# Last tile of a decoder layer: uneven gate columns, and a last norm shared by two engines and stored from two queues

## The reference, cut to what matters

```python
ffn = peer(x, ...)                                   # rows gathered from a table of 16384 experts
x = layer_norm(DEEPNORM_ALPHA * x + ffn, ln2_g, ln2_b)
gate = sigmoid(x @ ple_wgate + ple_bgate)            # 1024 x 1024
ple = gate * (p @ ple_wproj)                         # 256 x 1024
x = layer_norm(DEEPNORM_ALPHA * x + ple, ln3_g, ln3_b)
```

## Time and profile before

| what | us |
|---|---|
| time, median of 3 runs | 1459.02 (1455.46 to 1459.13) |
| the profiled execution, its time | 1458.8 |
| its span, first to last instruction | 1456.8 |
| mean granted TensorE clock | 0.886 |
| busy: PE / DVE / ACT / POOL | 1133.8 / 1084.4 / 934.7 / 602.7 |

### The profile page before, as it was taken

How to read it: one execution, slowest core, us unless ns; L and a number is a source line. 1 busy time by engine, 2 the same in 40 slices (tenths; PEclk the granted TensorE clock), 3 DMA queues, 4 the chain that set the end, 5 groups by cost and what they waited for, 6 DMA issues and landing times.

```text
span 1456.8 us, 18836 instructions
## 1 busy us (share of the span) xinstructions
PE 1133.8 (78%) x6787; PEld 889.4 (61%) x6787; DVE 1084.4 (74%) x2601; ACT 934.7 (64%) x1605; POOL 602.7 (41%) x533
## 2 busy tenths in 40 slices
PE   8999999988779877786666986777567775687666
PEld 3557777666667767665545565565555565566554
DVE  1388777769778886778747778877877787687867
ACT  2245678679878877766646666667655765666652
POOL 1034444334443434434424444554344444444551
PEclk9999999999889988898857988998879987778888
DMA  9589999999999999999999999999999999999991
GB/s 365 234 348 426 426 426 425 428 426 426 426 426 409 426 425 416 426 427 426 428 426 427 417 423 425 417 419 426 427 425 424 405 427 425 426 419 403 426 425 74
DMA packets 88359, 591.88 MB, mean 406 GB/s; under 512 B 9566, under 2 KB 14342, under 8 KB 19659
## 3 DMA queue, kind: packets, MB, share of 16 engines
q0 software_dynamic: 74128, 536.90, 88.0%
q1 hardware_dynamic: 14138, 53.79, 9.1%
HBM read 588.56 MB, written 2.10 MB: 405 GB/s over the span
## 4 chain that ended last, share of the span: by engine, by line
DMA 43%; PE 31%; ACT 10%; DVE 9%; POOL 3%; issue 3%; SPq 0%; POOLq 0%; DVEq 0%
DMA arena<-in_uv,ids 42%; PE ps L1051 12%; DVE arena L1609 6%; ACT arena L1256 5%; PE ps L763 4%; POOL arena L561 3%; PE ps L582 3%; PE ps L949 3%; PE ps L876 2%; ACT actv L1251 2%; PE ps L593 2%; ACT gel L1248 1%; ACT L1310 1%; ACT L1302 1%; PE ps L657 1%
## 5 line engine op out<-in xcount | busy, mean ns | idle before, releaser
L561 POOL DMA_INDIRECT arena<-in_uv,ids x512 | 589.8, 1152 | 787.3 <-PE ps L1051 664.4
L1051 PE MATMUL ps<-ident,arena 128*128 128x128 f32 x4076 | 618.9, 311 | 296.9 <-ACT arena L1256 296.0
L1051 PEld LDWEIGHTS ps<-ident,arena 128*128 128x128 f32 x4076 | 539.8, 161 | 395.3 <-ACT arena L1256 335.1
L1609 DVE CUSTOM_DVE_ANT_1 arena<-arena 128x1024 f32<-128x1024 f32 x384 | 468.5, 1225 | 207.5 <-DMA arena<-in_uv,ids 204.3
L1256 ACT ACTIVATE arena<-arena,actv 128x1024 f32<-128x1024 f32 x511 | 554.1, 1131 | 0.0
L1248 ACT ACTIVATE gel<-hid 128x2 f32<-128x2 f32 (+1 forms) x256 | 51.9, 203 | 406.7 <-DVE hid L1609 404.5
L1609 DVE CUSTOM_DVE_ANT_0 arena<-arena 128x1024 f32<-128x1024 f32 x128 | 155.4, 1224 | 63.3 <-DMA arena<-in_uv,ids 62.2
L1251 ACT ACTIVATE actv<-gel,gates 128x1 f32<-128x1 f32 x511 | 122.8, 287 | 8.4
L763 PE MATMUL ps<-arena 128*128 128x128 f32 x992 | 122.4, 285 | 0.0
L763 PEld LDWEIGHTS ps<-arena 128*128 128x128 f32 x992 | 120.5, 202 | 0.0
L876 PE MATMUL ps<-arena 128*128 128x384 f32 x192 | 65.9, 486 | 0.0
(11 more groups left out here) (226 smaller groups left out, 972.2 us busy)
## 6 DMA issues: line engine op xcount, KB each, us to landing
arena<-in_wq SPq DMA_DIRECT2D x20, 1024.0 KB, 9.0
arena<-in_uv,ids POOLq DMA_INDIRECT x517, 12.3
arena<-in_w_out SPq DMA_DIRECT2D x2, 2048.0 KB, 12.0
arena<-in_w_gate SPq DMA_DIRECT2D x1, 4096.0 KB, 17.9
arena<-in_w_out SPq DMA_DIRECT2D x3, 1024.0 KB, 13.5
arena<-in_w_k SPq DMA_DIRECT2D x4, 512.0 KB, 7.0
arena<-in_w_q SPq DMA_DIRECT2D x2, 1024.0 KB, 10.4
arena<-in_w_gv SPq DMA_DIRECT2D x1, 2048.0 KB, 12.0
```

The lines of the kernel that those rows point to most:

```text
L561: nc.gpsimd.indirect_dma_start(out=rows[:, c % RING, 0:n], out_offset=None, in_=a["uv"][:, :], in_offset=bass.IndirectOffsetOnAxis(ap=ids[ ...
L1051: i = mm(ps[:, run_bank(r) + k // 4, (k % 4) * P:(k % 4 + 1) * P], rows[:, c % RING, D + k * P:D + (k + 1) * P], ident[:, :], is_transpose ...
L1609: v.tensor_tensor_reduce(out=r, in0=r, in1=x1[t], scale=1.0, scalar=0.0, op0=ALU.mult, op1=ALU.add, accum_out=hid[:, i, c:c + 1]).then_inc ...
```

## The change: what it does

Three things, all in the tail of the last tile.

First, the four column groups of the gate, of 256 columns each, become groups of 320, 320, 256 and 128 columns (`LAST_COLS`), for the gate product, `gate_args`, the sigmoid and `add_embedding`. The instructions keep their number and order. The embedding is read through a view over two neighbouring banks, since columns 320 to 640 cross a bank's border.

Second, the last norm is cut at column 768 (`SPLIT`). VectorE centres columns 0 to 767 in one operation before it waits for the root, and rescales them in one operation after. GpSimd does columns 768 to 1023 in four operations, each waiting for the one before: subtract the mean and times g before the factor is known, times the factor and plus b after.

Third, the store: SyncE stores columns 0 to 767 in one transfer (384 KB), ScalarE's queue stores columns 768 to 1023 (128 KB), in place of SyncE's two of 512 columns (256 KB each).

```diff
--- before.py
+++ after.py
@@ -33,6 +33,8 @@
 
 RING = 8
 GRP = 2
+LAST_COLS = (0, 320, 640, 896, D)
+SPLIT = 768
 NG = TOPK // GRP
 HALF = D // 2
 REST = S - P
@@ -424,6 +426,12 @@
         ple_used = sem("ple_used")
         last_var = sem("last_var")
         last_root = sem("last_root")
+        last_mean_ready = sem("last_mean_ready")
+        last_rstd_ready = sem("last_rstd_ready")
+        last_centred = sem("last_centred")
+        last_kept = sem("last_kept")
+        last_a_ready = sem("last_a_ready")
+        last_b_ready = sem("last_b_ready")
         out_ready = sem("out_ready")
         out_done = sem("out_done")
 
@@ -512,8 +520,9 @@
             store(TAILS[1], 1)
             for u in range(28, NU):
                 load_wq(u)
-            for i in range(2, NT):
-                store(TAILS[i], i)
+            store(TAILS[2], 2)
+            sp.wait_ge(last_a_ready, 1)
+            sp.dma_start(out[0, TAILS[-1] * P:(TAILS[-1] + 1) * P, 0:SPLIT], x2[TAILS[-1]][:, 0:SPLIT]).then_inc(out_done, 16)
             sp.wait_ge(out_done, 2 * 16 * NT)
 
         @block.gpsimd
@@ -571,6 +580,17 @@
                     in_offset=bass.IndirectOffsetOnAxis(ap=ids[:, (NU - 1) % 4, c:c + 1], axis=0),
                     element_offset=PART,
                 ).then_inc(late_in[c - LATE], 16)
+
+            part = x2[TAILS[-1]][:, SPLIT:D]
+            pool.wait_ge(last_mean_ready, 1)
+            nc.gpsimd.tensor_scalar(part, part, aggr[:, 0:1], None, ALU.subtract).then_inc(last_centred, 1)
+            pool.wait_ge(last_centred, 1)
+            nc.gpsimd.tensor_tensor(part, part, ln3_g[:, SPLIT:D], ALU.mult).then_inc(last_centred, 1)
+            pool.wait_ge(last_centred, 2)
+            pool.wait_ge(last_rstd_ready, 1)
+            nc.gpsimd.tensor_scalar(part, part, rstd[:, 0:1], None, ALU.mult).then_inc(last_centred, 1)
+            pool.wait_ge(last_centred, 3)
+            nc.gpsimd.tensor_tensor(part, part, ln3_b[:, SPLIT:D], ALU.add).then_inc(last_b_ready, 1)
 
         @block.tensor
         def _(pe):
@@ -1073,7 +1093,7 @@
                         background(u * NG + c // 2)
 
             last = NT - 1
-            quarters = [(c * QD, (c + 1) * QD, (6, 7, run_bank(NR - 1), run_bank(NR - 1) + 1)[c]) for c in range(4)]
+            quarters = [(LAST_COLS[c], LAST_COLS[c + 1], (6, 7, run_bank(NR - 1), run_bank(NR - 1) + 1)[c]) for c in range(4)]
             pe.wait_ge(ple_used, 2 * last)
             pe.wait_ge(score_used, NU)
             pe.wait_ge(run_added, NR + 1)
@@ -1327,7 +1347,10 @@
                 if i == 0:
                     act.preload_act_table_set("sigmoid_and_others")
                     for c in range(4):
-                        gate_sigmoid(NT - 1, c, c * QD, (c + 1) * QD)
+                        gate_sigmoid(NT - 1, c, LAST_COLS[c], LAST_COLS[c + 1])
+
+            act.wait_ge(last_b_ready, 1)
+            act.dma_start(out[0, TAILS[-1] * P:(TAILS[-1] + 1) * P, SPLIT:D], x2[TAILS[-1]][:, SPLIT:D]).then_inc(out_done, 16)
 
         @block.vector
         def _(dve):
@@ -1366,7 +1389,11 @@
 
             def last_mean(n):
 
-                step(v.bn_aggr(aggr[:, :], stats[:, 0:n, :]))
+                if n == 4:
+                    v.bn_aggr(aggr[:, :], stats[:, 0:n, :]).then_inc(last_mean_ready, 1)
+                    dve.wait_ge(last_mean_ready, 1)
+                else:
+                    step(v.bn_aggr(aggr[:, :], stats[:, 0:n, :]))
                 v.tensor_scalar_add(var_e[:, 0:1], aggr[:, 1:2], EPS).then_inc(last_var, 1)
                 seen.inc(v.tensor_scalar(rtmp[:, 1:2], aggr[:, 1:2], EPS, -0.5, ALU.add, ALU.mult))
 
@@ -1377,7 +1404,12 @@
                 dve.wait_ge(last_root, i + 1)
                 step(v.reciprocal(y, root))
                 step(v.scalar_tensor_tensor(out=w, in0=y, scalar=minus_half, in1=y, op0=ALU.mult, op1=ALU.mult))
-                step(v.scalar_tensor_tensor(out=rstd[:, 0:1], in0=w, scalar=1.5, in1=y, op0=ALU.add, op1=ALU.mult))
+                last = v.scalar_tensor_tensor(out=rstd[:, 0:1], in0=w, scalar=1.5, in1=y, op0=ALU.add, op1=ALU.mult)
+                if i:
+                    last.then_inc(last_rstd_ready, 1)
+                    dve.wait_ge(last_rstd_ready, 1)
+                else:
+                    step(last)
 
             def centre(dst, src, g):
                 step(v.scalar_tensor_tensor(out=dst, in0=src, scalar=aggr[:, 0:1], in1=g,
@@ -1720,7 +1752,7 @@
                     dve.wait_ge(embedding_done, 2 * i + n + 1)
                 else:
                     dve.wait_ge(embedding_done, 2 * NT)
-                v.tensor_tensor(part, ps[:, bank, place:place + c1 - c0], part, ALU.mult).then_inc(ple_used, 1)
+                v.tensor_tensor(part, pair(bank)[:, place:place + c1 - c0], part, ALU.mult).then_inc(ple_used, 1)
                 dve.wait_ge(ple_used, 2 * i + n + 1)
                 step(v.scalar_tensor_tensor(out=dst, in0=dst, scalar=ALPHA, in1=part, op0=ALU.mult, op1=ALU.add))
                 half_stats(dst, chunk)
@@ -1844,12 +1876,17 @@
             y_rescale(last)
             for c in range(5):
                 if c < 4:
-                    gate_args(last, c, c * QD, (c + 1) * QD, (6, 7, run_bank(NR - 1), run_bank(NR - 1) + 1)[c])
+                    gate_args(last, c, LAST_COLS[c], LAST_COLS[c + 1], (6, 7, run_bank(NR - 1), run_bank(NR - 1) + 1)[c])
                 if c:
-                    add_embedding(last, c - 1, (c - 1) * QD, c * QD, free + (c - 1) // 2, (c - 1) % 2 * QD, c - 1)
+                    add_embedding(last, c - 1, LAST_COLS[c - 1], LAST_COLS[c], free, LAST_COLS[c - 1], c - 1)
             last_mean(4)
+            part = x2[TAILS[last]][:, 0:SPLIT]
+            v.scalar_tensor_tensor(out=part, in0=part, scalar=aggr[:, 0:1], in1=ln3_g[:, 0:SPLIT],
+                                   op0=ALU.subtract, op1=ALU.mult).then_inc(last_kept, 1)
             last_rstd(1)
-            normed_halves(x2[TAILS[last]], ln3_g, ln3_b, out_ready)
+            dve.wait_ge(last_kept, 1)
+            v.scalar_tensor_tensor(out=part, in0=part, scalar=rstd[:, 0:1], in1=ln3_b[:, 0:SPLIT],
+                                   op0=ALU.mult, op1=ALU.add).then_inc(last_a_ready, 1)
 
 
 # ---- launch: one core; the host only reorders axes ----
```

## The result

The changed kernel takes 1464.12 us (median of 6, 1463.48 to 1465.96), the kernel before 1458.01 us (median of 6, 1455.46 to 1459.13). The ratio is 1.0047, with a 95% interval of 1.0037 to 1.0057: slower, by 6.1 us from median to median and by 6.9 us by that ratio. The profiled execution took 1465.47 us with a span of 1463.7, against 1458.8 and 1456.8.

A forecast was written before the change was run, and what follows sets the result against it. Gathers, keeping DMA busy, pace the unchanged loop; in the last 27 us TensorE, then VectorE, then the final store count. Columns +0.80 and norm with stores -0.74 give +0.06 us: 1459.1 us, range 1455.3 to 1461.5.

The forecast's parts named there:

- Behind GpSimd's waits nothing is queued: Last norm and stores: GpSimd's late share delays nothing queued after it; at its upper price the end is A' + 6.75.
- A': Forecast start of the last norm's aggregate on VectorE: 0.80 us after the earlier 1450.01, at the upper end 1.24.
- The last rival: Tail: first uses of GpSimd arithmetic and ScalarE's store cost 1.65 us each, +4.6 in all, 1463.7; chance 0.06.
- Columns, +0.80: Last tile's uneven column groups: TensorE +0.87 us, VectorE -0.07, so the last aggregate starts 0.80 us later.
- c1's first half: TensorE, second column group of the last tile: 64 more columns at full clock cost +0.43 us.
- c0's: TensorE, first half of the first column group: 64 added columns cost +0.43 us at full clock, +0.87 at half.
- VectorE's norm, 3.02 us: Last norm on VectorE, aggregate's start to rescaling's end: 3.02 us in place of 4.42, a gain of 1.40.
- GpSimd's prices: GpSimd's last-norm share: 0.41 us per one-tensor operation, 0.64 per two-tensor one, 0.16 per hand-over; done at A' + 3.37.
- The upper price: GpSimd's last-norm operations at 1.15 us each, the mean of a gather's record; last result at about A' + 4.7.
- The rival of mutual exclusion: Last norm: VectorE operations with two SBUF inputs and GpSimd operations exclude each other, 1.15 us more, 1460.3; chance 0.20.
- the gain of 0.74: Last norm and its stores: the way from aggregate to end falls from 6.79 to 6.05 us.
- The stores: Two overlapping stores, 512 KB: some 0.66 us more than 256 KB; the end at A' + 6.05.

The follow-up runs named there:

- the first experiment: The changed kernel with GpSimd's four operations on columns 768 to 1023 given back to VectorE; uneven columns and two store queues stay: 1457.89 us, ratio to before 1.0001.

## Why the prediction was wrong

It forecast 1459.1, no change. The measured 1464.12 lies above the range, and slower by over 0.3% had a chance of 0.07.

- **The step that failed:** "Behind GpSimd's waits nothing is queued". The closing DRAIN was, and the path to the end ran through it and not through the stores. I followed what the profile counts as busy and priced a late engine by its operations alone. The runs show 7.7 us behind the end of GpSimd's last instruction, be it an addition or a memset; given back to VectorE, or drained early, the 6 us are gone. The line for it stood in the trace before, though hidden there; GpSimd did have something to do after its last gathers. So GpSimd's last result at A' + 3.37 was not the last that GpSimd had to do, and it was not true that the time could leave the range only if something outside the tail moved. The last rival had nearly the right time (1463.7) by luck, for a cause that isn't there: ScalarE's first transfer landed after 2.3 us, and the first arithmetic took 0.94 us as did the second multiplication when undisturbed.
- **Columns, +0.80:** measured +0.31 between the two profiles, and +0.79 between the kernel before and the run with the columns alone, where the clock rises at the same 3.8 us. c1's first half was as foreseen (+0.42 for +0.43), VectorE's part too (6.62 us from args(1) to the aggregate for 6.72, -0.10 for -0.07). In the changed kernel c0's was +0.03 for +0.43, since the clock rose after 2.8 us of TensorE's work and not 3.8. So the sum was right on its own condition, and the condition was a matter of chance: I had taken the moment of the rise as given. That c0's width costs nothing at full clock, where VectorE's late sum sets the pace, was in no case of mine.
- **VectorE's norm, 3.02 us:** measured 3.50 (1450.40 to 1453.90). Centring took 1.22 us and the Newton step 0.49; with GpSimd idle they are 1.01 and 0.22. These 0.48 us are the whole difference, the overlap with GpSimd that the forecast priced at nothing.
- **GpSimd's prices:** 0.41 and 0.64 us estimated, 0.94 and 0.72 measured undisturbed. With 1.69 for the held multiplication, its last result came 5.10 us after the aggregate, not 3.37, and with it ScalarE's store. The upper price had also been added up wrong: with 1.15 us for each of the four, the first pair ends at A' + 2.89, behind the factor, and the last result comes at A' + 5.5, not 4.7.
- **The rival of mutual exclusion:** right in mechanism for two of the three pairs of operations above, and set too low at 0.20. The 0.2 us of overlap in the earlier trace rows were too short to speak against it: the select may have been held for just the 0.06 us that it took longer. The order differed from my working: GpSimd's subtraction came first by 0.07 us, so it was VectorE's centring that took longer. Norm and stores without the DRAIN came to +0.5 us (7.28 for 6.79), where this rival had +0.41 (1.15 less the gain of 0.74).
- **The stores:** near. With both queues at work together, in the first experiment, they landed 2.4 and 2.3 us after their issue, and the end came 3.1 us after VectorE's first rescaling for 3.03. In the changed kernel they did not overlap, for GpSimd's share was late.

## What to carry to other kernels

Before giving an idle engine a share of the last work, look at what it still has to do after it: ask the trace for the closing line of the block with each sequencer's DRAIN, not for busy time. On GpSimd, after the 517 gathers of this kernel, that is 7.7 us behind its last operation; let its last instruction end so long before the end, or clear it with an early DRAIN while nobody waits. Price work that GpSimd and VectorE do at the same time as if they took turns where VectorE reads two SBUF tensors: here the held operations cost 0.21, 0.27 and 0.75 us. And before a step is summed at one clock, work it out at the other too: the same columns cost 0.3 us or 0.8.

## What the runs showed of the hardware

- GpSimd's closing DRAIN grows by about 0.082 us for each indirect gather (0.174, 0.269, 0.848, 5.43 us after 0, 1, 8, 64), alike for rows of 4 and 8 KB and for 3.5 or 24 us between the last gather and the end. It took 5.11 us after 512, of which 60 lie behind the last of four pauses of 1.6 us that come every 113 gathers, and 7.80 us after the 517 of the large kernel, 86 of them behind its last such pause. A DRAIN of its own ahead of it clears it: the closing one then ends 0.1 us after GpSimd's last operation.
- A GpSimd multiplication of 128x256 float32 by a scalar takes 0.94 us alone, and 1.69 when a VectorE operation with two SBUF inputs is 0.13 us ahead of it; VectorE's 128x768 centring took 1.22 us in place of 1.01 with GpSimd's subtraction 0.07 us ahead of it, and its 128x1 Newton step 0.49 in place of 0.22 beside GpSimd's product.
- TensorE's granted clock rose from 0.50 to 1.00 at 3.8 us after the tail's gate product began in the execution before, and at 2.8 us in the one after, with TensorE at work without a gap from the product's start in both; over all traces it rose between 2.8 and 4.3 us after that start, or was full before it. After, in busy time by stretch with the clock as third number from the end:

```profile
1432.20:1432.40 0.20, 0.20 (x2) 0.04 (x1) 0.20 (x1) 0.00 (x0) 0.00 (x0) 0.57 0.00 0
```
